# GLA stage of a mixer kernel: scores, band, items and outputs of the same step on TensorE, with the last head's tail folded in

## What is computed

```python
logits = einsum(glr, gla_w_gate) + gla_b_gate            # per direction, head
log_a = log_sigmoid(logits) / GLA_TAU
# per direction, head, chunk of 64 tokens:
cum = cumsum(log_a); last = cum[-1]
q_dec, k_inv, k_end = q * exp(cum), k * exp(-cum), k * exp(last - cum)
scores = where(mask, q_dec @ k_inv.T, 0)
o = scores @ v + q_dec @ S_start
S_end = exp(last) * S_start + k_end.T @ v
# per head, forward plus backward direction:
on = (o - mean(o)) * rsqrt(var(o) + 1e-5)
y_gla = on * gla_norm_g * silu(r)
```

## Time and profile before

| | us |
|---|---|
| median of 3 runs | 3422.35 |
| lowest to highest | 3421.32 to 3430.11 |
| the profiled execution | 3430.41 |
| its span, first to last instruction | 3428.6 |
| TensorE busy | 3026.7 (88%) |
| VectorE busy | 1913.3 (56%) |
| ScalarE busy | 1025.7 (30%) |
| GpSimd busy | 905.7 (26%) |
| mean granted TensorE clock | 0.93 |

### The profile page before, as it was taken

The page is one execution under the profiler, slowest core; times in us unless marked ns, Lnnn a source line. Parts: engine busy times, 40 slices in busy tenths (PEclk is TensorE's granted clock), DMA queues, the critical chain, the costliest instruction groups (busy, mean ns, idle before and its releaser), DMA issues. The chain is left out here.

```text
span 3428.6 us, 43505 instructions
## 1 busy us (share of the span) xinstructions
PE 3026.7 (88%) x17520; PEld 2906.8 (85%) x17520; DVE 1913.3 (56%) x2226; ACT 1025.7 (30%) x1573; POOL 905.7 (26%) x433
## 2 busy tenths in 40 slices
PE   7999987986969786979999699999939999999994
PEld 7999987865758576979998689999929999999993
DVE  7667762333333436679999441355476555555556
ACT  2777782222322323224444310100141111010112
POOL 1122111100100001145452333333313334443330
PEclk9999998977979688989999899999969999999996
DMA  5222312000100003343433442422201111111111
GB/s 224 75 82 93 111 43 64 22 17 14 43 13 24 24 14 100 137 153 109 127 113 101 165 147 90 141 102 87 82 25 38 43 43 43 43 37 43 43 37 55
DMA packets 107843, 254.08 MB, mean 74 GB/s; under 512 B 20352, under 2 KB 51072, under 8 KB 107584
## 3 DMA queue, kind: packets, MB, share of 16 engines
q1 hardware_dynamic: 97920, 212.18, 19.6%
q10 hardware_dynamic: 9792, 40.11, 3.2%
HBM read 195.86 MB, written 56.37 MB: 74 GB/s over the span
## 5 line engine op out<-in xcount | busy, mean ns | idle before, releaser
L2354 PE MATMUL bank<-yhi,mrg_hi 128*128 128x384 f32 x1056 | 356.6, 338 | 31.3 <-POOL mrg_lo L167 21.3
L2354 PE MATMUL bank<-yhi,mrg_lo 128*128 128x384 f32 x1056 | 355.0, 336 | 0.0
L2354 PE MATMUL bank<-ylo,mrg_hi 128*128 128x384 f32 x1056 | 355.0, 336 | 0.0
L1708 PE MATMUL bank<-hhi,s_hi 128*128 128x384 f32 x768 | 265.4, 346 | 21.6 <-POOL s_lo L180 18.4
L950 PE MATMUL bank<-hhi,gla_hi 128*128 128x384 f32 x600 | 221.4, 369 | 49.8 <-POOL gla_lo L180 35.6
L164 POOL TENSOR_TENSOR mlp_hi<-mlp_raw,zero 128x1024 fp32r<-128x1024 f32 x64 | 121.8, 1903 | 534.7 <-PE bank L2681 225.9
L2681 PE MATMUL bank<-ahi,mlp_hi 128*128 128x384 f32 x768 | 257.4, 335 | 3.5 <-DVE alo L2730 3.5
L1708 PE MATMUL bank<-hhi,s_lo 128*128 128x384 f32 x768 | 259.2, 338 | 0.0
L1708 PE MATMUL bank<-hlo,s_hi 128*128 128x384 f32 x768 | 258.7, 337 | 0.0
L2681 PE MATMUL bank<-ahi,mlp_lo 128*128 128x384 f32 x768 | 256.6, 334 | 0.0
L2681 PE MATMUL bank<-alo,mlp_hi 128*128 128x384 f32 x768 | 256.5, 334 | 0.0
(11 more groups left out here) (395 smaller groups left out, 7852.9 us busy)
## 6 DMA issues: line engine op xcount, KB each, us to landing
mlp_raw<-in_mlp_units SPq DMA_DIRECT2D x64, 512.0 KB, 3.5
ada<-in_w_ada SPq DMA_DIRECT2D x32, 512.0 KB, 3.6
s_raw<-in_s_units SPq DMA_DIRECT2D x32, 512.0 KB, 4.5
mid_gates<-gate ACTq DMA_DIRECT2D x24, 576.0 KB, 3.2
gt<-mid_gates SPq DMA_DIRECT2D x24, 576.0 KB, 3.8
gla_raw<-in_gla_units SPq DMA_DIRECT2D x25, 512.0 KB, 3.6
lru_raw<-in_lru_units SPq DMA_DIRECT2D x24, 512.0 KB, 6.8
mid_s_tab<-tabq SPq DMA_DIRECT2D x8, 1152.0 KB, 7.6
```

The costliest lines, as they stand in the source:

```text
L1708: mm = pe.matmul(out, wts[par][:, w], r[:, k, cols], start=(k == 0 and x == 0), stop=(k == KD - 1 and x == 2))
L2354: mm = pe.matmul(out, wt[par][:, w], r[:, slot, cols], start=(k == 0 and n == 0), stop=(k == len(order) - 1 and n == 2))
```

## The change

`turn_items`, `TAIL_BANDS` and the tail loops go. On TensorE a step is scores(s), band, items, outputs(s). v is transposed pair by pair, from step 10 of the head before to step 0. The norm of head h - 1 moves to steps 6 to 11 of head h, and each of its pieces on VectorE and ScalarE stands a step behind the item it needs; advance and collect come first in each step on VectorE. `keys` and `queries` are one and two steps later, k is projected ahead of q, and a new semaphore `k_free` lets k's bank be emptied after `keys`. In head 3 the bands of its own r come in steps 0 to 5 (their silu goes into `v`, which is free then) and those of head 2's r in steps 8 to 13; its norm begins in step 13, from the last third of the tokens, which the backward direction ends first. `y` is stored in six pieces a head, each 192 KB, as they become ready. The diff, cut to its core:

```diff
+        VALUES = [[(0, 1), (2, 3), (4, 5), (6, 7), (8,)]] + [[(0,)] + [(n,) for n in range(NPAIR - 1, 0, -1)]] * LAST
+        FREED_AT = {n: s for s, (d, n) in enumerate(STEPS) if d}
...
+            HEAD_UNIT.append(len(UNITS))
+            if h < LAST:
+                UNITS += [("v", h + 1, 0), ("v", h + 1, 1), ("k", h + 1, 0), ("q", h + 1, 0)]
+            else:
+                UNITS += [("r", LAST, 0), ("r", LAST, 1)]
             if h:
                 UNITS += [("r", h - 1, 0), ("r", h - 1, 1)]
-            HEAD_BANDS.append(range(first, NB * len(UNITS)))
-        TAIL_BANDS = range(NB * len(UNITS), NB * len(UNITS) + 2 * NB)
-        UNITS += [("r", HEADS - 1, 0), ("r", HEADS - 1, 1)]
...
+        def norm_band(h, i):
+            return i if h < LAST else NB - 1 - i
 
         def step_band(h, s):
 
-            at = s if h else (s if s < 12 else None)
-            if h + 1 == HEADS:
-                at = s - 12 if s >= 12 else None
-            return [] if at is None else [HEAD_BANDS[h][at]]
+            first = NB * HEAD_UNIT[h]
+            if h == LAST:
+                return [first + s] if s < 6 else [first + s - 2] if 8 <= s < 14 else []
+            return [first + s] if h or s < 12 else []
...
         def step_items(h, s):
 
             got = []
             if s == 0:
-                got.append(("gate", h, 1, 2))
-            if h and 1 <= s <= NB:
-                got.append(("mean", h - 1, 0, s - 1))
-            if h and 4 <= s < 4 + NB:
-                got.append(("var", h - 1, 0, s - 4))
+                if h:
+                    got.append(("value", h, 0, NPAIR - 1))
+                got.append(("gate", h, 1, 0))
+            if s == 1:
+                got += [("gate", h, 1, 1), ("gate", h, 1, 2)]
             if 7 <= s < 7 + NB:
                 got.append(("key", h, 1, s - 7))
-            if h + 1 < HEADS:
+            if h < LAST:
+                if s == 0 and h:
+                    got.append(("key", h, 0, 2))
                 if s == 9:
                     got += [("gate", h + 1, 0, 0), ("gate", h + 1, 0, 1)]
                 if s == 10:
                     got.append(("gate", h + 1, 0, 2))
-                if s >= 15:
-                    got.append(("key", h + 1, 0, s - 15))
+                if s >= 10:
+                    got.append(("value", h + 1, 0, s - 10))
+                if s >= 16:
+                    got.append(("key", h + 1, 0, s - 16))
+            else:
+                if s == 0:
+                    got.append(("key", h, 0, 2))
+                if s in (13, 16):
+                    got.append(("mean", h, 0, (s - 13) // 3))
+                if s == 15:
+                    got.append(("var", h, 0, 0))
+            if h and 8 <= s < 8 + NB:
+                got.append(("var", h - 1, 0, s - 8))
+            if h and 6 <= s < 6 + NB:
+                got.append(("mean", h - 1, 0, s - 6))
             return got
...
-                def store_y(h):
-                    sync.wait_ge(y_done, h + 1)
-                    sync.dma_start(dram["y_gla"][2 * h + 2:2 * h + 4].rearrange("a p n -> p a n"), o[h % 2][:]).then_inc(y_out, 16)
+                def store_y(h, j):
+                    w, b = (SILU if h < LAST else SILU_LAST)[j]
+                    cols = slice(b * BW, (b + 1) * BW)
+                    sync.wait_ge(rm_done, 2 * NB * h + j + 1)
+                    sync.dma_start(dram["y_gla"][2 * h + 2 + w][:, cols], o[h % 2][:, w, cols]).then_inc(y_out[b], 16)
...
-                    first = HEAD_BANDS[h][0] // NB
+                    first = HEAD_UNIT[h]
+                    store_final(h, 0)
                     load(first + 2)
+                    if h >= 2:
+                        store_y(h - 2, 2 * NB - 1)
                     load(first + 3)
-                    store_final(h, 0)
-                    if h >= 2:
-                        store_y(h - 2)
-                    if h + 1 < HEADS:
+                    if h < LAST:
                         load(first + 4)
                         load(first + 5)
-                    store_final(h, 1)
-                    if h + 1 < HEADS:
+                        store_final(h, 1)
                         load_cached(h + 1)
-                    for u in range(first + 6, HEAD_BANDS[h][-1] // NB + 3):
-                        load(u)
-                store_y(HEADS - 2)
-                store_y(HEADS - 1)
-                sync.wait_ge(y_out, 16 * HEADS)
+                        if h:
+                            load(first + 6)
+                            load(first + 7)
+                            for j in range(2 * NB - 1):
+                                store_y(h - 1, j)
+                    else:
+                        for j in range(2 * NB):
+                            if j == 2:
+                                store_final(h, 1)
+                            store_y(h - 1, j)
...
-                    if s == 0:
-                        pe.wait_ge(free_act, FREED[ITEM["value", h, 0, NVT - 1]][1])
-                    if s >= NPAIR and (n == 0 or n % 3 == 2):
+                    if d == 0:
+                        pe.wait_ge(free_act, FREED[ITEM[last_value(h, s)]][1])
+                        if n % 3 == 0:
+                            pe.wait_ge(free_act, FREED[ITEM["key", h, 0, PIECES[0].index(n // 3)]][1])
+                    elif n == 0 or n % 3 == 2:
...
+                    item(key)
                 for h in range(HEADS):
-                    pe.wait_ge(band_free, 5 * NB if h == 0 else HEAD_BANDS[h - 1][2 * NB])
-                    for key in turn_items(h):
-                        item(key)
-                    scores(h, 0)
                     for s in range(NSTEP):
-                        if s + 1 < NSTEP:
-                            scores(h, s + 1)
+                        scores(h, s)
...
-                for x in range(NB):
-                    band(TAIL_BANDS[x])
-                    item(TAIL_MEANS[x])
-                band(TAIL_BANDS[NB])
-                for x in range(NB):
-                    item(TAIL_VARS[x])
-                for x in (4, 5):
-                    band(TAIL_BANDS[x])
+                for key in TAIL:
+                    item(key)
...
+                    elif h == LAST:
+                        act.wait_ge(item_mm, ITEM["value", h, 0, NPAIR - 1] + 1)
+                        ins = act.activation(v[:, w, cols], src, ACT.Silu)
...
-                        if h and x == 0:
-                            act.wait_ge(o_mm, NSTEP * h)
-                        n = min(2, NPAIR - 2 * x)
-                        ins = act.activation(vt[:, 2 * x:2 * x + n, :],
+                        group = VALUES[h][x]
+                        n0, n = group[0], len(group)
+                        if h:
+                            act.wait_ge(o_mm, NSTEP * (h - 1) + FREED_AT[n0] + 1)
...
                             evac_item(key)
-                        if s == 0:
+                        if s == 1:
                             log_gates(h, 1)
-                        if h and 2 <= s < 2 + NB:
-                            square(h - 1, s - 2)
                         if s == 4:
                             decays(h, 1)
-                        if h + 1 < HEADS:
+                        if h and 7 <= s < 7 + NB:
+                            square(h - 1, s - 7)
+                        if h < LAST:
                             if s == 10:
                                 log_gates(h + 1, 0)
                             if s == 13:
                                 decays(h + 1, 0)
-                for x in range(2):
-                    evac_band(TAIL_BANDS[x])
-                    square(HEADS - 1, x)
-                square(HEADS - 1, 2)
-                for x in range(NB):
-                    evac_item(TAIL_VARS[x])
-                for x in range(2, 2 * NB):
-                    evac_band(TAIL_BANDS[x])
+                        elif s in (14, 17):
+                            square(h, (s - 14) // 3)
+                evac_item(TAIL[0])
+                square(LAST, 2)
+                evac_item(TAIL[2])
 
...
+                        if h and 8 <= s < 8 + NB:
+                            spread(h - 1, s - 8)
+                        if h and 7 <= s < 7 + NB:
+                            centre(h - 1, s - 7)
+                        if h and 6 <= s < 6 + NB:
+                            total(h - 1, s - 6)
+                        if s == 3:
+                            forget(h, 1)
+                        if s == 4:
+                            accumulate(h, 1)
+                        if s == 6:
+                            keys(h, 1)
+                            ended(h, 1, 0)
+                        if s == 7:
+                            ended(h, 1, 1)
+                            queries(h, 1)
+                        if s == 8:
+                            ended(h, 1, 2)
+                        if h and 9 <= s < 9 + NB:
+                            normalise(h - 1, s - 9)
```

(83 more changed lines are left out.)

102 lines of the change are left out of this document (58 added, 44 removed).

## The result

The kernel became faster: 3254.3 us median (3251.97 to 3254.85), against 3426.2 us for the kernel before on the same chip (3421.32 to 3431.47). The ratio is 0.9497, with a 95% interval of 0.9478 to 0.9515. The forecast took 137 us off a profiled execution; measured against each other, the two profiled executions differ by 178.4 us (3430.41 to 3251.97).

A forecast was written before the change was run, and what follows sets the result against it. TensorE was the engine to follow, but latency, its waits for VectorE, the loss. Gains of 2 + 46 + 49 + 38.5 + 1.5 = 137 us took the profiled 3430.41 to 3293, median 3285; range 3263 to 3313, 3319 with nearer rivals.

The forecast's parts named there:

- head 0: First GLA head, without bands in steps 12 to 17: 7 + 1 - 5.6 - 0.7 = 2 us gained.
- head 1: Second GLA head: 187.4 us less 38.9 idle and 14.4 lower clock, some losses added: 141, a gain of 46.
- head 2: Third GLA head: from 187.7 to 138.5 us, a gain of 49.
- head 3 up to the last product: Fourth GLA head with its long norm tail: 149 us against 187.6 before, 38.5 gained.
- The cover: In steps with a 4.28 us band, VectorE may reach advance at most 2.8 us late without delaying outputs.
- The small stalls: Waits the new order adds: mean 2 in step 8 about 1.1 us, the key item in step 0 about 0.3.
- the term for the falls of the clock: TensorE's clock falls in item groups between bands: three falls counted, 3.1 us each; head 1 was charged 3 for one.
- 0.61 us per clean step: TensorE's wait ahead of scores for VectorE's collect, in steps without mean or variance items: 0.61 us goes in every step.
- Rival 2: Clean steps keep their 0.6 us because VectorE's tail ends later than the cover allows: 36 us, 3321; chance 0.07.
- The last chain: End of head 3 after its last scores, from advance and collect through the remaining norm to the last products: 18.6 us.
- (1): The clock falls in most item groups between bands; at 15 falls 37 us higher, 3322; chance 0.09.
- 3 and 4: VectorE's holds delay outputs: 82 us slower, 3504, chance 0.03; or another wait takes over, nothing gained: 3422, chance 0.02.

The follow-up runs named there:

- run 12: The changed kernel repeated with no edit, beside three of the follow-up kernels: 3252.05 us, 0.9503 of the kernel before.
- 10: The changed kernel with three unused sums of 128x384 on VectorE ahead of each step's copy of the scores in heads 1 and 2: 3262.6 us, 0.9528.
- 11: The changed kernel with six unused sums of 128x384 on VectorE in each step of heads 1 and 2: 3307.0 us, 0.9653.
- 1: The changed kernel with only TensorE's order undone, scores again a step ahead of outputs: 3294.1 us, 0.9615.
- 3: The changed kernel with both undone: scores a step ahead on TensorE, and VectorE held in centre and normalise: 3392.0 us, 0.99.
- 2: The changed kernel with centre and normalise back in the step that issues their item, so VectorE waits inside the step: 3256.4 us, 0.9507.
- 4: The changed kernel with head 0's 12 bands moved to steps 2 to 8 and 11 to 15: 3247.8 us, 0.9484.
- 5: The changed kernel with head 3's 12 bands moved to steps 3, 6, 7 and 8 to 16: 3242.0 us, 0.9464.
- 6: The changed kernel with the bands of heads 0 and 3 both moved, without filling matmuls: 3232.3 us, 0.9444.
- Experiment 7: The changed kernel with unread 128x384 matmuls filling TensorE's waits in steps without a band: 3239.1 us, 0.9452.
- 8: The changed kernel with the bands of heads 0 and 3 moved and the remaining waits filled with unread matmuls: 3226.3 us, 0.9415.
- 9: The changed kernel with head 3's own r and norm put back behind its steps, head 2's r bands in steps 12 to 17: 3277.3 us, 0.9569.

## Why the prediction missed, by its own steps

The terms, each against what was measured between the same events:

| term | predicted gain, us | measured |
|---|---|---|
| head 0 | 2 | 13.7 |
| head 1 | 46 | 55.0 |
| head 2 | 49 | 55.2 |
| head 3 up to the last product | 38.5 | 48.6 |
| last store to the next stage | 1.5 | 2.4 |
| sum | 137 | 174.9 |

The stages behind gave another 3.5 us that no edit touches, and up to 608 us the two differ by less than 1 us. In run 12 head 0 ends 6.7 us earlier, head 3 takes 3.2 us longer up to the last product (142.15 against 138.98), and the stages behind take 2.1 us longer: the terms of heads 0 and 3 are good to some 6 and 3 us, those of heads 1 and 2 to 0.1.

**Right.** The idle time ahead of scores goes and nothing takes its place. The cover is confirmed by 10 and 11, at 2.95 to 2.98 us for the 2.8 of the sum. The small stalls were put at 1.4 us in head 1; the mean item waits 0.9 and the variance item 0.3. ScalarE's two table loads per variance item stayed inside the second band bank. The outputs wait about a round trip only where no band lies between: 1.0 to 1.3 us in head 0.

**Failed: the term for the falls of the clock.** Three falls in item groups (9.3 us) were counted in, 2.5 us for carrying the lower level into head 1, and the lower level in all of head 0's last six steps. None of these falls came in the middle heads. A group like that of the earlier trace rows, four and a half microseconds of small matmuls between two bands:

```profile
797.00:801.59 4.59, 4.59 (x25) 2.71 (x23) 0.29 (x1) 3.90 (x6) 0.00 (x0) 1.00 0.00 2
```

It has no idle time in it and stays at full clock. The two windows of the earlier trace rows had shown one fall and one stay in the kernel before, with 0.60 and 0.61 us of idle time, and I put the fall down to the small matmuls. In before, in 1, 3 and 11 the clock fell in or behind some such groups that came with idle time. With the new order on TensorE no fall began between the turn to head 1 and the turn to head 3 in any of ten profiled executions (after, 2, 4 to 10 and 12). The change took the idle time away, and with it the falls. The sum did let the falls behind long waits go with their waits (14.4 us in head 1); the step that failed is that it kept falls in item groups as if they had a cause of their own, 3 of the 9.0 us by which head 1 was better and 3 of the 6.2 in head 2. The 2.5 us for the lower level carried into head 1 are chance: in after it ended at the turn (725.20), in the profiled executions of 2 and 5 it reached 4.4 and 5.9 us into head 1. In head 0 the first three steps without a band still ran at full clock, at 3.8 to 4.2 us a step where 6.2 was counted for all but the first:

```profile
696.22 0.44 PE L1032 MATMUL bank<-qd,ki 128*128 128x128 f32 x2
...
698.68 0.49 PE L1052 MATMUL bank<-probs,vt 128*128 128x128 f32 x2 [1.02 <-DVEq L1306]
...
700.07 0.44 PE L1032 MATMUL bank<-qd,ki 128*128 128x128 f32 x2
...
702.59 0.49 PE L1052 MATMUL bank<-probs,vt 128*128 128x128 f32 x2 [1.07 <-DVEq L1306]
...
706.74 0.49 PE L1052 MATMUL bank<-probs,vt 128*128 128x128 f32 x2 [1.32 <-DVEq L1306]
...
708.12 0.72 PE L1032 MATMUL bank<-qd,ki 128*128 128x128 f32 x2
```

The clock fell only at 708.14, after three waits of 1.0 to 1.3 us (in brackets) in a row; the last three steps took 5.9, 5.9 and 5.4 us. In run 12 the same waits brought no fall, so these waits do not by themselves decide it. Head 0 took 6.1 us less there than in after, so the 13.7 of the table could as well have been some 20. With the fall in steps 9 and 10 that was kept in the sum (3.1 us) and did not come, this and the overlap of the next point (some 2 us), this is the 11.7 us by which head 0 was better, within 1 us. The same holds in head 3: steps 8, 14 and 15 took 8.5, 3.85 and 6.6 us, where 10.7, 4.5 and 8.7 were counted, 4.95 us together.

**Failed: 0.61 us per clean step.** The distance from scores to scores fell from 7.35 to 6.58, by 0.77. From the outputs' start to the next scores' start it is now 1.29 us (759.72 to 761.01 above). Before, the outputs alone had 1.45 us, up to the end of their last matmul (896.57 to 898.02), and then the wait began that ended at 898.62:

```profile
896.57 0.38 PE L1016 MATMUL bank<-probs,vt 128*128 128x128 f32 x2
...
897.46 0.56 PE L1020 MATMUL bank<-qd,state 128*128 128x64 f32 x4
```

Now their last matmuls overlap the next scores. That is 0.16 us in each step, 3 us in a head, which a wait hides in the profile of before and which goes with it. The prediction's own step of 6.55 us was right; its sum for head 1 took off the idle time alone and so did not agree with it.

**Failed: the range.** The range reached 22 us down, of which 9 were for the clock. The sum held more of the clock than that: 9.3 in the heads, 2.5 at the turn, and the lower level in head 0 and head 3. Experiment 7, in which all of it went up to 1110 us, came to 3239. The rivals had only the side on which the clock falls more often; none had the side on which it stops falling.

**Smaller slips in the sums.** Six steps of 6.2 us are 37.1, not 36.5. Rival 2 counted 60 times 0.6 us where it named 54 steps. Neither moves the forecast by 1 us.

**Head 3, to the end.** The last chain was predicted at 18.6 us and took 17.0. On VectorE (in brackets the idle time and what ended it):

```profile
1115.47 0.41 DVE L1281 TENSOR_TENSOR o<-o,bank 128x256 f32<-128x256 f32 x1
...
1119.41 0.95 DVE L1331 TENSOR_TENSOR o<-o,bank 128x768 f32<-128x768 f32 x1 [2.46 <-PE bank L1011]
...
1126.85 1.15 DVE L1347 SCALAR_TENSOR_TENSOR o<-o,gla_params,gla_scale 128x384 f32<-128x384 f32 x2 [3.40 <-ACT gla_scale L1151]
1128.15 1.03 DVE L1358 TENSOR_TENSOR o<-o,v 128x384 f32<-128x384 f32 x2
```

Before, 49.8 us lay between the last collect and the last product; now it is 13.7 (1115.47 to 1129.18).

None of the four rivals came: the clock does not fall in the groups (1), VectorE's tail is inside the cover (2, by 10 and 11), its holds cost nothing measurable as long as scores do not need the newest collect (3 and 4, by experiment 2).

## What to carry to other kernels

When two engines pass work back and forth, look first at which result each step asks for: a wait for the newest result of an engine that also waits inside its step costs far more than either alone (40 and 2 us, 138 together). Taking away the wait for the newest result was enough here: 2 us were left, within the noise, while taking away only the holds would have left 40. Where idle time and a lower clock stand in the same steps, cost them as one loss, and let the low end of the range assume that both go. A stretch that must wait can be given work: moved bands were worth 20 to 22 us here, unread matmuls 15, and both 28. Before a fall of the clock in one profile is put down to an edit, profile the same kernel a second time.

## What the runs showed of the hardware

The granted clock did not fall for small matmuls as such. 8.3 and 8.8 us without a large block passed at full clock with 0.65 and 0.18 us of idle time in them (4; the first had 1.14 us more of idle time 0.8 us ahead of it), while groups with 0.56 to 2.0 us of idle time in or close before them sometimes fell (1), and with unread matmuls in the waits there was no fall between 560 and 1110 us (7). The same steps with the same waits (1.02, 1.07 or 1.08, 1.32 us) fell in the profiled execution of after and did not in that of run 12. So the idle time of a pattern does not settle alone whether the clock falls; something that differs from one execution to the next has a say in it. What decides stays open: only whole patterns were varied.

VectorE and GpSimd slow each other down. Three sums of 128x384 on VectorE took 1.75 us alone and 3.29 beside GpSimd's split of 2.38 us; two rows of experiment 10's VectorE:

```profile
742.58 3.29 DVE L1294 TENSOR_TENSOR pad<-hhi,hlo 128x384 bf16<-128x384 f32 x3 [2.98 <-PE bank L1039]
...
807.88 1.75 DVE L1294 TENSOR_TENSOR pad<-hhi,hlo 128x384 bf16<-128x384 f32 x3 [3.88 <-PE bank L1039]
```

The split beside the first starts at 741.89; there is none beside the second. The Trainium skill (GPSIMD Engine Reference, 1. Specifications) says that the two contend when VectorE reads two inputs from SBUF; the trace agrees, and puts the price at 1.54 us for a split here. The price is about the time that the split still has to run. It ends at 744.27, 1.69 us after the sums begin. In experiment 11 a split that ends 0.82 us after the sums begin costs them 0.67 (4.20 against 3.53 us), and in the earlier trace rows one that ends 2.25 us after the scan begins costs it 2.11 (4.66 against 2.55). Each loss is the overlap less 0.15 us. In these three places the split had begun first, and it took its usual 2.36 to 2.38 us. Where a split began 0.22 us behind the start of such sums (814.90 in experiment 10) it took 2.59 us itself, and the sums 3.82.
